# First gathers of rows ahead of the second network's constants, and the eighth weight piece held for the first gather

## The reference

```python
for l in range(DEPTH):
    ...
    h = h + gt1 * merge_branches(...)
    xn2 = modulate(rms_norm(h, g_norm_ffn[l]), sh2, sc2)
    y = hier_moe(xn2, ...)            # 2 of 32 experts per token
    h = h + gt2 * y

def expert_block(args):
    xb, e = args
    hdn = jax.nn.silu(xb @ w_gate[e]) * (xb @ w_up[e])
    return hdn @ w_down[e]
```

## Time and profile before

| | |
|---|---|
| median of 3 runs | 2942.62 us |
| lowest and highest | 2940.2, 2942.9 us |
| profiled execution, its own time | 2936.96 us |
| its span | 2935.2 us |
| TensorE matmul busy | 86% of the span |
| VectorE, ScalarE, GpSimd busy | 25%, 16%, 6% |
| mean granted TensorE clock | 0.953 |
| DMA | 666.35 MB, 227 GB/s over the span |

### The profile page before, as it was taken

One profiled execution on the slowest core, in us unless ns is written; L12 is line 12 of the kernel. 1 busy time (PEld: TensorE's weight loads), 2 busy tenths in 40 slices (PEclk: granted clock), 3 DMA queues, 4 the chain that ended last, 5 costly groups with the idle time before them and its releaser, 6 DMA issues.

```text
span 2935.2 us, 29768 instructions
## 1 busy us (share of the span) xinstructions
PE 2529.7 (86%) x11962; PEld 1532.2 (52%) x11962; DVE 723.3 (25%) x1443; ACT 466.6 (16%) x1011; POOL 171.8 (6%) x194
## 2 busy tenths in 40 slices
PE   5999999998887777469999969777757899998998
PEld 2444545544444444235577635344435568885873
DVE  1575443114200000144143220000002302312221
ACT  2111222201010000022122101010002021202320
POOL 0000000000111111000000011111100000000000
PEclk8999999998999999889999979999988998999999
DMA  7354010324899999817323489999992232243341
GB/s 301 148 215 175 35 58 29 143 86 164 367 425 426 426 426 424 361 62 286 115 87 115 188 362 423 425 426 426 425 390 73 107 143 86 82 158 147 143 148 53
DMA packets 59973, 666.35 MB, mean 227 GB/s; under 512 B 12772, under 2 KB 12932, under 8 KB 20704
## 3 DMA queue, kind: packets, MB, share of 16 engines
q1 hardware_dynamic: 44592, 630.48, 52.8%
q0 software_dynamic: 14416, 31.30, 2.9%
q10 hardware_dynamic: 864, 3.15, 0.3%
HBM read 664.81 MB, written 21.02 MB: 234 GB/s over the span
## 4 chain that ended last, share of the span: by engine, by line
PE 59%; DMA 25%; issue 9%; DVE 4%; ACT 1%; POOL 0%; SPq 0%; POOLq 0%; DVEq 0%; ACTq 0%
DMA branches<-in_w_moe 15%; PE act_bank L629 7%; PE act_bank L639 7%; PE act_bank L710 5%; PE act_bank L1044 4%; PE vec_bank L726 4%; PE vec_bank L874 4%; PE score_bank L710 4%; PE vec_bank L710 3%; PE score_bank L952 3%; PE vec_bank L962 3%; DMA heads<-in_w_moe 3%; DMA xT<-in_w_moe 3%; DMA values<-in_w_moe 2%; PE vec_bank L952 2%
## 5 line engine op out<-in xcount | busy, mean ns | idle before, releaser
L629 PE MATMUL act_bank<-ring,xT 128*128 128x512 f32 x448 | 195.1, 596 | 2.1 <-DVE xT L1798 1.1
L639 PE MATMUL act_bank<-xT,ring 128*128 128x512 f32 (+1 forms) x512 | 194.4, 541 | 0.0
L2119 DVE TENSOR_TENSOR heads<-work,vec_bank 128x256 f32<-128x256 f32 x64 | 26.9, 421 | 543.8 <-PE vec_bank L952 543.8
L710 PE MATMUL act_bank<-xT,ring 128*128 128x256 f32 (+1 forms) x576 | 157.7, 427 | 1.8 <-ACT branches L1305 1.1
L639 PEld LDWEIGHTS act_bank<-xT,ring 128*128 128x128 f32 x512 | 97.4, 191 | 95.8 <-issue 91.9
L952 PE MATMUL score_bank<-ring,branches 128*64 128x256 f32 x1024 | 120.8, 389 | 30.6 <-issue 17.7
L629 PEld LDWEIGHTS act_bank<-ring,xT 128*128 128x128 f32 x448 | 85.2, 191 | 107.8 <-issue 107.8
L962 PE MATMUL vec_bank<-ring,heads 128*64 128x512 f32 x512 | 116.9, 598 | 28.2 <-DMA ring<-in_w_moe 23.0
L952 PE MATMUL vec_bank<-ring,branches 128*64 128x256 f32 x1024 | 117.2, 381 | 26.7 <-DMA ring<-in_w_moe 26.7
L710 PEld LDWEIGHTS act_bank<-xT,ring 128*128 128x128 f32 x576 | 109.2, 190 | 44.0 <-issue 31.1
L726 PE MATMUL vec_bank<-branches,ring 128*128 128x256 f32 (+1 forms) x416 | 125.6, 445 | 0.0
(11 more groups left out here) (369 smaller groups left out, 3330.3 us busy)
## 6 DMA issues: line engine op xcount, KB each, us to landing
ring<-in_w_moe SPq DMA_DIRECT2D x96, 2048.0 KB, 36.9
ring<-in_w_in SPq DMA_DIRECT2D x31, 2048.0 KB, 8.4
ring<-in_w_merge SPq DMA_DIRECT2D x27, 2048.0 KB, 8.1
ring<-in_w_ada SPq DMA_DIRECT2D x24, 2048.0 KB, 8.5
branches<-in_w_moe SPq DMA_DIRECT2D x24, 2048.0 KB, 36.9
heads<-in_w_moe SPq DMA_DIRECT2D x24, 2048.0 KB
xT<-in_w_moe SPq DMA_DIRECT2D x24, 2048.0 KB
values<-in_w_moe SPq DMA_DIRECT2D x24, 2048.0 KB, 36.7
```

The costliest lines, as they stand in the source:

```text
L629: mm = pe.matmul(b.t[:, 0:n], xT[:, k, tile * P:(tile + 1) * P], w[:, k * COLS + c0:k * COLS + c0 + n], start=(k == 0), stop=(k == KD - 1))
L639: mm = pe.matmul(b.t[:, 0:n], w[:, k * COLS + f * P:k * COLS + (f + 1) * P], xT[:, k, 0:n], start=(k == 0), stop=(k == KD - 1))
L710: mm = pe.matmul(g.t[:, 0:n], merge_tile(l, i, MERGE_TILES * d + k), xs[:, k, 0:n], start=(k == 0), stop=(k == KD - 1))
```

## The change

In GpSimd's queue the four constants of block 1 are issued after the first two gathers instead of ahead of them. In SyncE's queue the eighth piece waits, in both blocks, also for the first gather to have landed. `gathered[0]` rises by 16 with every even expert, so in block 1 the first gather is the 17th of that buffer.

```diff
@@ gpsimd @@
         def experts(l):
             gather(l, 0)
             gather(l, 1)
+            if l == DEPTH - 1:
+                second_block_early()
             for e in range(N_EXP):
...
             dispatch(l)
-            if l == DEPTH - 1:
-                second_block_early()
             experts(l)
...
@@ sync, load_home @@
             elif home == 3:
                 sp.wait_ge(x_stored[l], 16 * tiles(l))
+                sp.wait_ge(gathered[0], 16 * (N_EXP // 2 * l + 1))
             sp.dma_start(ring[NSLOT + home][:, 0:SLOT], source(c)).then_inc(ring_loaded[NSLOT + home], 16)
```

## The result

The changed kernel takes 2935.27 us (7 runs, 2930.33 to 2937.01) against 2942.62 before. The ratio is 0.9973 with a 95% interval of 0.9962 to 0.9984, so it is 0.27% faster, 7.35 us by the medians; forecast were 8.2. In a second measurement it took 2935.57 against 2941.72, ratio 0.9983 (0.9973 to 0.9992). The ratios are estimated from all single executions, so they are not quite the quotients of the medians: 0.9973 is 7.9 us, 0.9983 is 5.0.

A forecast was written before the change was run, and what follows sets the result against it. Expert stages were taken as bound by DMA engines that stay full from the ninth weight piece on. Gains of 1.4 us (block 0) and 6.8 (block 1) sum to 8.2, from 2942.62 to 2934.4 us; range 2931.5 to 2940.0, forecast's own 2931.5 to 2936.8.

The forecast's parts named there:

- What bounds the stage: Expert stages: DMA engines never rest after the ninth piece starts, so moving that start by x moves the end by x.
- fourth rival: Expert stages: nothing moves because the end hangs on something other than the ninth piece's start; 2942.6 us, chance 0.04.
- Block 0, the gather alone on the engines: Block 0's first gather: without the eighth piece beside it, it lands in 3.3 instead of 4.66 us, gaining 1.4.
- Block 1, the gather: Block 1's first gather: issued 1.9 us earlier and taking 3.0 instead of 7.90 us, gaining 6.8, bounds 5.1 to 7.1.
- TensorE's clock: First up product, both blocks: no change taken; half clock would cost 1.8 and 1.1 us, full clock gain 1.7 and 2.4.
- What the profile after would show: Expected profile signs, among them the ninth piece 1.4 us earlier in block 0 and 6.8 in block 1 from the table.
- My sign of being wrong: One of the signs against the prediction: a first up product longer than 6 us.
- The cover of the held piece: Gap from gather landing to ninth piece: block 1's held piece and constants need 6.8 of 7.9 us; hold costs nothing.
- first rival: Block 1: held piece and constants spill over the ninth piece, losing 2 to 3 us; 2937.4 us, chance 0.14.
- Second rival: First gather stays at 4.66 us in both blocks; block 0 gains nothing, block 1 5.1; 2937.5 us, chance 0.12.
- Third rival: Block 1: VectorE's list holds the gather's descriptors until 1710.8, so the gain there is 2.1 us; 2939.1 us, chance 0.04.
- Fifth rival: Both blocks: held piece, with the constants, stands wholly ahead of the ninth piece; 9.8 us slower, 2952.4 us, chance 0.06.

The follow-up runs named there:

- ninth_late: The changed kernel with the ninth piece also held until expert 0's second up product is done: 2942.00 us, ratio 1.0006 to the kernel before.
- order_only: The kernel before with only the constants moved behind the first two gathers, the eighth piece not held: 2937.02 us, ratio 0.9988.
- hold_only: The kernel before with only the eighth piece held for the first gather, the constants still ahead of the gathers: 2937.42 us, ratio 0.9985.
- after_again: The changed kernel measured once more, nothing altered: 2935.57 us, ratio 0.9983 to the kernel before.
- hold_two: The changed kernel with the seventh piece held for the first gather too: 2940.77 us, ratio 0.9995 to the kernel before.
- hold_to_issue: The changed kernel plus 12 matmuls and constants at stage end, eighth piece held only until the first gather is issued: 2940.78 us, ratio 0.9999 to before.
- hold_to_second: The changed kernel plus 12 matmuls and constants at stage end, eighth piece held only until the second gather is issued: 2946.86 us, ratio 1.0021 to before.

## Why the prediction was right

**What bounds the stage.** Right. The end follows the ninth piece one for one (ninth_late, order_only, hold_only), so the fourth rival, in which nothing moves, is out.

**Block 0, the gather alone on the engines: 1.4 us.** It measured 4.66 - 3.31 = 1.35. The stage kept 0.8 of it, because the first up product grew by 0.66.

**Block 1, the gather: 6.8 us.** The landing moved from 10.69 to 3.78 after the table, 6.9. The stage kept 6.2; the up product grew by 0.77. So the mis-sized term is the one that I set to zero: "TensorE's clock", which took back 1.4 us in the profiled pair. With it the ninth piece came 0.7 and 6.1 us earlier, not the 1.4 and 6.8 of "What the profile after would show". In the changed kernel, its repetition and the other kernels with the landing hold but no added matmuls, block 0's gather lands after 4.1 to 4.3 us and the product takes 5.76 to 5.83. With a landing after 5.5 (before, order_only) it takes 5.14 and 5.17. In block 1 it is 6.58 and 5.94 against 5.81. That the granted clock does it is shown by the runs with the added matmuls: 3.67 in both blocks, at a granted clock of 1.00 against 0.54. What decides how long the clock stays low is not shown. It is not the length of the wait alone: with a landing after 6.9 and 8.8 us block 1's product takes 5.06 and 5.09 (hold_only, order_only), with one after 10.7 it takes 5.81. My bounds (1.8 and 1.1 of loss) held the loss. My sign of being wrong, a first up product over 6 us, came true in block 1 (6.58) all the same. The sign was set tighter than the bounds, which reached 6.9, and it pointed at the right term.

**The sum.** 8.2 forecast, 0.8 + 6.2 = 7.0 in the stages of the profiled pair, 0.5 + 5.6 = 6.1 in the repetition, and 7.35 and 6.2 by the medians. By the ratios it is 7.9 and 5.0. All but the last are inside the forecast's own range (5.8 to 11.1). The gathers were sized well, and the sum is about 1 us too high because nothing was taken off for the clock.

**The cover of the held piece: 6.8 of 7.9 us in block 1.** The conclusion was right, the size not. From 1709.37, just ahead of the landing (1709.45), to 1718.67, just ahead of the ninth piece's first bytes, the queues of the changed kernel show, over 9.3 us:

```profile
q1 hardware_dynamic: 143, 2.10, 53.8%
q0 software_dynamic: 363, 0.79, 35.3%
```

The piece took 0.538 x 9.3 = 5.0 us of all engines, as counted. The constants and the rest of GpSimd's took 0.353 x 9.3 = 3.3 and not the 1.9 of their bytes: 363 packets for 0.79 MB against 143 for 2.10. Together that is 8.3, and the gap was 8.6. The room of 1.0 us was in truth 0.3, and even this only because the slow first product had widened the gap. That it fitted was luck. Where the product was shorter (after_again, a gap of 8.0) the time from ninth piece to end is 1.3 longer. That was my first rival. It happened there in part, it happened in full with the added matmuls, and with the constants out of the gap 1.5 and 0.2 us of it were left.

**Second rival, a gather that stays at 4.66 beside the rest of the backlog.** It did not happen, and my price for it was taken from the wrong row. In block 0 the gather of before took 4.66 because 4.3 us of backlog lay ahead of it. At the same moment of block 1 it was 8, and the gather took 7.96 (order_only). Where the hold does not clear the queue, the landing moves by 1.9 us only and the stage by 2.7, against the 5.1 that I called the lower bound.

**Third rival, VectorE's list.** The gather of block 1 was issued at 1706.48, under the list, and landed in 2.97, against 2.7 for the one that I took as free of everything. The port rule of the Trainium skill, "SBUF — State Buffer", section "SBUF: two separate sides", costs nothing visible here; the operations of this list work on one partition and are short (0.17 and 0.16 us the first and the last). Whether any of them takes the port, no run tells.

**Fifth rival, a held piece that is not covered.** Not in the changed kernel, but hold_two shows that it is real: one piece more, and the gain is gone.

## What to carry to other kernels

Here small transfers on the critical path that shared the DMA engines with bulk loads landed with the bulk's backlog, as long as this was no more than some 8 us. It pays to clear the queue ahead of them, by holding back a load that has slack; issuing them sooner pays in full only then. Holding the load until they had landed worked, holding it until they were issued lost all of the gain, and nothing in between was tried; what is held must fit in the time until the next load is due, counted by the engines' share and not by bytes. If that time is filled by work that TensorE starts after idling, the gain may be eaten by its clock; here a few matmuls ahead of it, with the constants out of the gap, took the ratio from 0.9973 and 0.9983 to 0.9960 twice.

## What I had not expected of the hardware

A gather of at most 256 KB (64 rows of 4 KB) took 2.8 to 3.7 us where the weights were held and no constants stood ahead, and 7.93 to 8.56 when one 2 MB load was issued some 0.14 us before or 0.4 us after it. The load itself took 8.1 us from issue to landing in hold_to_issue and 8.0 in hold_to_second, where the gather had been issued first.

In an expert stage with the weight queue always full, the gathers of the changed kernel land in a median of 9.7 us and 11.2 at most, although pieces of weights take 36.9. So with a deep queue the wait is well below the whole backlog; no run here tells what sets it.

A semaphore that GpSimd raises behind a DMA in its program does not wait for the 1.1 us that the profile shows GpSimd busy with that DMA. With it behind the first gather, SyncE issued the piece 0.13 us before the profile shows that gather's start; with it behind the second, 1.04 us before the second's start (742.88 and 743.92).
